# Value products of the first mixer with the values stationary and two heads in column tiles, probabilities divided before the product, and compression in four quadrants of TensorE

## What is computed

```python
p = _split_columns(u @ w_in)                                  # proj blocks and gate blocks
o_a = _stick_breaking(q_a, k_a, v_a)                          # 4 heads: w @ v, w = exp(...) below the diagonal
o_b = _dsa_attention(...)                                     # 4 heads: softmax over the top keys, p @ v_b
o_c = _nsa_attention(...)                                     # 4 heads, three value products, each with a gate:
#   gb[...,0:1] * o_cmp + gb[...,1:2] * o_sel + gb[...,2:3] * o_win
def _compress(tok, pos_emb, w1, w2):                          # for keys and for values, 15 windows of 32 tokens
    hid = gelu(blocks.reshape(B, n_cmp, CMP_LEN * hd) @ w1)   # (15 x 2048) @ (2048 x 128)
    return hid @ w2
def _masked_softmax(s, mask):
    ...
    return e / jnp.maximum(den, 1e-30)
merged = g[0] * (o_a @ w_up[0]) + g[1] * (o_b @ w_up[1]) + g[2] * (o_c @ w_up[2])
return merged @ w_out
```

## Time and profile before

| | us |
|---|---|
| median of 3 runs | 751.03 (749.55 to 751.15) |
| the profiled execution | 750.67 |
| its span | 748.6 |
| PE busy | 741.5 (99%) |
| DVE busy | 601.3 (80%) |
| ACT busy | 376.7 (50%) |
| POOL busy | 30.6 (4%) |

### The profile page before, as it was taken

How to read it: one execution, slowest core, us unless ns; L and a number is a source line. 1 busy time by engine, 2 the same in 40 slices (tenths; PEclk the granted TensorE clock), 3 DMA queues, 4 the chain that set the end, 5 groups by cost and what they waited for, 6 DMA issues and landing times.

```text
span 748.6 us, 14960 instructions
## 1 busy us (share of the span) xinstructions
PE 741.5 (99%) x6348; PEld 732.2 (98%) x6348; DVE 601.3 (80%) x897; ACT 376.7 (50%) x506; POOL 30.6 (4%) x22
## 2 busy tenths in 40 slices
PE   8999999999999999999999999999999999999998
PEld 8999999999999999999999999999999999999998
DVE  4756889899897778998998888979788886687554
ACT  6558255654666543443434666266556553434330
POOL 0000000004000000000000000301110000000000
PEclk9999999999999999999999999999999999999999
DMA  8844373332743459999887526655344565688511
GB/s 334 310 155 154 110 281 113 109 126 102 309 177 138 158 185 365 361 333 338 324 310 276 181 102 225 226 184 210 112 169 142 198 226 176 228 278 303 199 57 57
DMA packets 24113, 156.07 MB, mean 208 GB/s; under 512 B 3568, under 2 KB 3696, under 8 KB 6000
## 3 DMA queue, kind: packets, MB, share of 16 engines
q1 hardware_dynamic: 24048, 155.13, 57.7%
HBM read 154.07 MB, written 1.05 MB: 207 GB/s over the span
## 4 chain that ended last, share of the span: by engine, by line
PE 95%; DVE 2%; DMA 1%; ACT 1%; issue 1%; SPq 0%; DVEq 0%
PE bank L803 17%; PE bank L804 16%; PE bank L805 16%; PE bank L886 9%; PE bank L888 9%; PE bank L889 9%; PE bank L811 3%; PE bank L813 3%; PE bank L814 3%; PE bank L1294 2%; PE bank L1261 1%; DMA sb_raw<-in_stream 1%; PE bank L1271 1%; PE bank L1191 1%; PE bank L1335 0%
## 5 line engine op out<-in xcount | busy, mean ns | idle before, releaser
L1770 DVE TENSOR_TENSOR sb_lo<-sb_raw,sb_hi 128x2048 fp32r<-128x2048 f32 (+1 forms) x114 | 259.2, 2277 | 72.7 <-ACT sb_hi L1425 72.4
L1425 ACT CAST sb_hi<-sb_raw 128x2048 fp32r<-128x2048 f32 (+1 forms) x114 | 215.5, 1895 | 99.6 <-PE bank L889 49.6
L803 PE MATMUL bank<-sb_u_hi,sb_hi 128*128 128x256 f32 (+1 forms) x688 | 193.1, 281 | 0.0
L805 PE MATMUL bank<-sb_u_hi,sb_lo 128*128 128x256 f32 (+1 forms) x688 | 190.5, 277 | 0.0
L804 PE MATMUL bank<-sb_u_lo,sb_hi 128*128 128x256 f32 (+1 forms) x688 | 190.5, 277 | 0.0
L803 PEld LDWEIGHTS bank<-sb_u_hi,sb_hi 128*128 128x128 f32 (+1 forms) x688 | 128.9, 187 | 2.8 <-issue 2.2
L804 PEld LDWEIGHTS bank<-sb_u_lo,sb_hi 128*128 128x128 f32 (+1 forms) x688 | 129.2, 188 | 0.0
L805 PEld LDWEIGHTS bank<-sb_u_hi,sb_lo 128*128 128x128 f32 (+1 forms) x688 | 129.0, 187 | 0.0
L886 PE MATMUL bank<-sb_hid_hi,sb_hi 128*128 128x256 f32 x432 | 119.3, 276 | 0.0
L888 PE MATMUL bank<-sb_hid_lo,sb_hi 128*128 128x256 f32 x432 | 119.2, 276 | 0.0
L889 PE MATMUL bank<-sb_hid_hi,sb_lo 128*128 128x256 f32 x432 | 119.2, 276 | 0.0
(11 more groups left out here) (370 smaller groups left out, 1335.4 us busy)
## 6 DMA issues: line engine op xcount, KB each, us to landing
sb_raw<-in_stream SPq DMA_DIRECT2D x140, 1024.0 KB, 5.2
sb_raw<-in_stream SPq DMA_DIRECT2D x4, 256.0 KB, 6.4
sb_raw<-in_stream SPq DMA_DIRECT2D x2, 512.0 KB, 9.0
sb_mem_t<-in_mem SPq DMA_DIRECT2D x1, 1024.0 KB, 4.8
out<-sb_h SPq DMA_DIRECT2D x4, 256.0 KB, 2.2
sb_const<-in_constants SPq DMA_DIRECT2D x1, 830.0 KB, 11.1
sb_h<-in_x SPq DMA_DIRECT2D x1, 572.0 KB, 3.8
sb_h<-in_x SPq DMA_DIRECT2D x1, 512.0 KB, 6.7
```

The source lines that it names most:

```text
L803: nc.tensor.matmul(out, a_hi, b_hi, start=(i == 0), stop=False)
L805: last = nc.tensor.matmul(out, a_lo, b_hi, start=False, stop=(i == n - 1))
L1425: nc.scalar.copy(place(hi, s)[:, 0:n], x[:, 0:n]).then_inc(sem("hi_ready"), 1)
L1770: tt(place(lo, s)[:, 0:n], x[:, 0:n], f32(place(hi, s)[:, 0:n]), ALU.subtract) \
```

## The change

The table of constants gets `pick`, 16 columns that add the right 16 columns of each 32-row quadrant. Six things change.

1. `pv_stick` runs once for a pair of heads, the values (64 columns) stationary and the weights moving, head 0 into rows 0 to 63 and head 1 into rows 64 to 127 of bank 2, so that the result has features on partitions.
2. `pv_pair(u)` replaces `pv(u)` and `pv(u + 1)` of branches b and c in the same way; the compressed branch (`cmp_pv`) is added into the same bank. `o_group` 0 to 4 and the transposes of `turn_o` go; `turn_o` is now a scaled copy from the bank on ACT and one DVE instruction.
3. The probabilities are divided before they are turned: POOL inverts the sums (and multiplies by the gate for branch c), ACT scales the two halves of each unit.
4. The exponentials, the division and the transposes of a pair of units move into the gate block behind their scores, and `pv_pair` stands right behind that block.
5. `turn_cmp_p` moves from inside gate 7 to behind gate 7, in front of `scores` 8 and 9, and has one more DVE instruction (the division).
6. `cmp_product` is one step with w1 moving (128 columns) and 32 columns of windows stationary, step k in quadrant k mod 4. ACT copies the 128x128 result (`cmp_parts`), and `cmp_sum` adds the quadrants with one product with `pick`. The evacuation of gate 2 moves behind `cmp_product(0)`.

```diff
     block("proj", 7, between=[("suffix", 1)])
-    steps([("pv_stick", 0), ("stick", 2)])
+    steps([("stick", 2)])
...
-    steps([("pv_stick", 1), ("stick", 3), ("split", "gate", 1)])
+    steps([("pv_stick", 0), ("stick", 3), ("split", "gate", 1)])
...
-    steps([("pv_stick", 2), ("split", "gate", 3), ("turn_cmp", 0)])
-    block("gate", 2, between=[("pv_stick", 3), ("o_group", 0), ("turn_cmp", 1), ("index", 0), ("rope1", 3)])
-    steps([("cmp_product", 0, 0)])
-    block("gate", 3, between=[("cmp_product", 0, 1), ("cmp_hidden", 0), ("topk", 0, 0)])
-    steps([("cmp_product", 1, 0), ("topk", 0, 1), ("turn_qk", 2)])
-    block("gate", 4, between=[("cmp_product", 1, 1), ("cmp_hidden", 1), ("cmp_hid",), ("topk", 0, 2)])
+    steps([("split", "gate", 3), ("turn_cmp", 0)])
+    block("gate", 2, evac_now=False, between=[("pv_stick", 2), ("turn_o", 0), ("turn_cmp", 1), ("index", 0), ("rope1", 3)])
+    steps([("cmp_product", 0)])
+    evac(where["gate", 2])
+    block("gate", 3, between=[("cmp_sum", 0), ("cmp_hidden", 0), ("topk", 0, 0)])
+    steps([("cmp_product", 1), ("topk", 0, 1), ("turn_qk", 2)])
+    block("gate", 4, between=[("cmp_sum", 1), ("cmp_hidden", 1), ("cmp_hid",), ("topk", 0, 2)])
...
-    steps([("scores", 4), ("scores", 5), ("topk", 0, 3), ("turn_o", 0)])
+    steps(unit_scores(4) + unit_norms(4) + [("topk", 0, 3)])
     block("gate", 6, ahead=False, between=[("cmp_scores",), ("rounds", "gate", 8)])
-    steps([("turn_p", 4), ("turn_p", 5), ("scores", 6), ("scores", 7)])
-    block("gate", 7, ahead=False, between=[("pv", 4), ("pv", 5), ("turn_cmp_p",), ("split", "gate", 8), ("topk", 1, 0), ("turn_qk", 6)])
-    steps([("turn_p", 6), ("turn_p", 7), ("scores", 8), ("scores", 9), ("topk", 1, 1), ("split", "gate", 9)])
-    block("gate", 8, ahead=False, evac_now=False, between=[("cmp_pv",), ("o_group", 1)])
-    steps([("rounds", "gate", 10), ("pv", 6), ("pv", 7), ("turn_p", 8), ("turn_p", 9), ("scores", 10), ("scores", 11)])
+    steps(unit_scores(6))
+    block("gate", 7, ahead=False, between=unit_turns(4) + unit_norms(6) + [("split", "gate", 8), ("topk", 1, 0), ("turn_qk", 6)])
+    steps([("pv_pair", 4), ("turn_cmp_p",)] + unit_scores(8) + [("topk", 1, 1), ("split", "gate", 9)])
+    block("gate", 8, ahead=False, evac_now=False, between=unit_turns(6) + unit_norms(8) + [("cmp_pv",)])
+    steps([("rounds", "gate", 10), ("pv_pair", 6)] + unit_scores(10))
...
-    block("gate", 11, ahead=False, evac_now=False, between=[("pv", 0), ("pv", 1)])
-    steps([("rounds", "up", 2), ("turn_p", 2), ("turn_p", 3)])
+    block("gate", 11, ahead=False, evac_now=False, between=unit_turns(0) + unit_norms(2))
+    steps([("rounds", "up", 2), ("pv_pair", 0)])
     evac(where["gate", 11])
+    add("turn_o", 2)
     split(where["up", 2])
-    block("up", 0, ahead=False, between=[("merge", 0, 0), ("merge", 0, 1), ("pv", 2), ("pv", 3), ("turn_o", 2),
-                                         ("merge", 0, 2), ("split", "up", 1), ("merge", 0, 3)])
-    block("up", 2, ahead=False, between=[("merge", 1, 0), ("merge", 1, 1), ("rounds", "out", 0), ("turn_o", 1)])
+    block("up", 0, ahead=False, between=[("merge", 0, 0), ("merge", 0, 1)] + unit_turns(2) +
+          [("merge", 0, 2), ("split", "up", 1), ("merge", 0, 3)])
+    steps([("pv_pair", 2), ("turn_o", 1)])
+    block("up", 2, ahead=False, between=[("merge", 1, 0), ("merge", 1, 1), ("rounds", "out", 0)])
...
-            def pv_stick(hd):
+            def pv_stick(first):
...
+                for kt in range(NT):
+                    out, w = (slice(at, at + T), slice(0, T)) if kt == 0 else (slice(at + P, at + T), slice(T, T + P))
+                    for hd in (first, first + 1):
+                        r, c = slice(HD * (hd % 2), HD * (hd % 2) + HD), VA + HD * hd
+                        last = nc.tensor.matmul(ps[r, out], proj[:, kt, c:c + HD], prob[:, hd % 2, w],
+                                                start=(first == kt == 0), stop=(kt == 1), skip_group_check=True)
...
+            def cmp_product(i):
...
+                for k in range(16):
+                    r = slice(32 * (k % 4), 32 * (k % 4) + 32)
+                    pair = 16 * (k - k % 2)
+                    last = nc.tensor.matmul(ps[r, 0:P], cmp_in[:, i, pair:pair + 32], w[:, k, :], start=(k < 4),
+                                            stop=(k >= 12), skip_group_check=True)
+                fill(last, key)
+
+            def cmp_sum(i):
+
+                wait_evacuated(pe, ("cmp_parts", i))
+                ps = claim(("cmp_hidden", i), "turn")
+                fill(nc.tensor.matmul(ps[:, 0:16], cmp_parts[:, i, :], cst("pick"), start=True, stop=True),
+                     ("cmp_hidden", i))
...
+            def pv_pair(u):
...
+                for n, (s, kt) in enumerate(parts):
+                    for x in (u, u + 1):
+                        i = UNITS[x][2]
+                        r = slice(HD * (i % 2), HD * (i % 2) + HD)
+                        p = prob_t_of(x)[:, 0:2 * keys * P].rearrange("p (m k q) -> p m k q", m=2, k=keys)
+                        if kind == "b":
+                            out = ps[r, :].rearrange("p (m t q) -> p m t q", m=2, t=NT)[:, :, t, :]
+                            v, p = proj[:, kt, VB:VB + HD], p[:, :, kt, :]
+                        else:
+                            out = ps[r, i // 2 * T + t * P:i // 2 * T + t * P + P]
+                            v, p = proj[:, kt, (VSEL, VWIN)[s]:(VSEL, VWIN)[s] + HD], p[:, s, kt, :]
+                        last = nc.tensor.matmul(out, v, p, start=(opens and n == 0), stop=(n == len(parts) - 1),
+                                                skip_group_check=True)
...
+            def cmp_product(i):
+
+                key = ("cmp_parts", i)
+                ps = wait_filled(act, key)
+                free(nc.scalar.copy(cmp_parts[:, i, :], ps[:, 0:P]), key)
...
+            def norm_p(u):
+
+                n = P * (UNITS[u][1] + 1)
+                act.wait_ge(sem("rden_ready"), EXP_ORDER[u] - 3)
+                for m in range(2):
+                    x = prob_of(u)[:, m * n:m * n + n]
+                    last = nc.scalar.activation(x, x, ACT.Copy, scale=rden[:, u, m:m + 1])
+                last.then_inc(sem("p_ready"), 1)
...
             def turn_o(c):
-                turn_to((turned_hi[:, :, :], u_hi[:, 2:4, :], u_hi[:, 4:6, :])[c], ("turn_o", c))
+
+                act.wait_ge(sem("pv_done"), (4, 16, 12)[c])
+                if c == 2:
+                    wait_filled(act, ("block", where["gate", 11]))
...
                 link(tt(cmp_d[:, :], cmp_d[:, :], gate_c[:, :, :, 0].rearrange("p t h -> p (t h)"), ALU.mult))
+                heads = p.rearrange("p (h n) -> p h n", n=32)
+                tt(heads, heads, over(cmp_d[:, :], 32), ALU.mult).then_inc(sem("cmp_p_ready"), 1)
```

More of the change, by code:

```diff
@@ L177, in steps @@
             else:
-                if step[0] == "cmp_product" and step[2] == 0:
+                if step[0] == "cmp_product":
                     raw.append(("cmp_w1", step[1]))
@@ L280, in plan @@
+    block("gate", 8, ahead=False, evac_now=False, between=unit_turns(6) + unit_norms(8) + [("cmp_pv",)])
+    steps([("rounds", "gate", 10), ("pv_pair", 6)] + unit_scores(10))
     evac(where["gate", 8])
     steps([("split", "gate", 10), ("topk", 1, 2)])
-    block("gate", 9, ahead=False, evac_now=False, between=[("pv", 8), ("pv", 9)])
-    steps([("rounds", "gate", 11), ("turn_p", 10), ("turn_p", 11), ("scores", 0), ("scores", 1)])
+    block("gate", 9, ahead=False, evac_now=False, between=unit_turns(8) + unit_norms(10))
@@ L284, in plan @@
+    steps([("rounds", "gate", 11), ("pv_pair", 8)] + unit_scores(0))
     evac(where["gate", 9])
     steps([("split", "gate", 11), ("topk", 1, 3)])
-    block("gate", 10, ahead=False, evac_now=False, between=[("pv", 10), ("pv", 11)])
-    steps([("rounds", "up", 0), ("turn_p", 0), ("turn_p", 1), ("scores", 2), ("scores", 3)])
+    block("gate", 10, ahead=False, evac_now=False, between=unit_turns(10) + unit_norms(0))
+    steps([("rounds", "up", 0), ("pv_pair", 10)] + unit_scores(2))
     evac(where["gate", 10])
@@ L1225, in cmp_pv @@
                 wait_evacuated(pe, ("turn_cmp_p",))
-                ps = claim(("o", 1), O_BANK[1])
-                for t in range(NT):
-                    last = nc.tensor.matmul(ps[:, t * T:t * T + T], cmp_in[:, 1, t * P:t * P + P], vc_bd,
-                                            start=True, stop=True)
-                fill(last, ("o", 1))
+                ps = banks[lease["turn_o", 2][0]]
+                for m in range(2):
+                    nc.tensor.matmul(ps[:, m * T:m * T + T], vc_bd[:, m * P:m * P + P], cmp_in[:, 1, :],
+                                     start=False, stop=False, skip_group_check=True)
             def scores(u):
@@ L1272, in turn_p @@
                 fill(last, ("turn_p", u))
+            def pv_pair(u):
+                kind, t, _ = UNITS[u]
```

(31 more changed lines are left out.)

146 lines of the change are left out of this document (71 added, 75 removed).

## The result

| | us |
|---|---|
| median of the changed kernel, 4 runs | 755.9 (755.32 to 756.81) |
| median of before, its runs on the same chip | 750.48 (749.55 to 751.15) |
| ratio | 1.0084, 95% interval 1.0069 to 1.0098 |
| span of the profiled execution | 754.0, before 748.6 |

The change makes the kernel slower by 0.84% (the two medians are 5.4 us apart, a quotient of 1.0072; what is given in us for a ratio further down is worked out from the ratio, 0.84% being 6.3 us). The forecast was 750.5, no change, with a range up to 753.7.

What follows compares the result with a forecast made beforehand. PE, 99% busy, was to wait for ACT and DVE at three points, so out 0 starts 0.5 us earlier: 750.67 less 0.5 is 750.2, plus the median's 0.36 gives 750.5 us, range 747.4 to 753.7.

Steps and rivals of the forecast that it cites:

- A: At `cmp_sum(1)` in gate 4: PE waits about 4 us for ACT's copy behind gate 3's tanh, keeping 0.45 us saved.
- B: At `turn_cmp_p` ahead of gate 8: PE waits 2.3 us for DVE, and gate 8 starts 0.6 us later than before.
- the 0.5 of the sticks: Part of the stick products' saving, 0.5 us, counted toward PE's earlier arrival at `cmp_sum(1)`.
- Column pairs: Value products in two column tiles, priced like row pairs of the scores: 0.65 us for first queries, 1.09 for second.
- Scalings on ACT: Division of the probabilities on ACT, two scalings for each unit, taken at 0.42 us a scaling.
- the clock falls: Rival, 10 of 100: the waits at A and B bring the 1.2 GHz level for half a block, 753.4 us.
- the clock reads below 1.00 behind A: Sign of being wrong: granted clock under full speed after the wait at `cmp_sum(1)`, where the forecast had 1.00.
- Point C: From up 0 to out 0: ACT's late copy for `turn_o(2)` delays DVE's merge; out 0 starts 0.5 us earlier.
- the 3.2 saved: PE's saving after gate 8: 2.34 us of value products and 0.88 us of two `turn_o`.
- Column tiles that take turns: Rival, 15 of 100: products in different column tiles do not run together, so the kernel takes 753.5 us.
- Weight loads not hidden: Rival, 8 of 100: 0.106 us for each of 26 column-tile passes behind B, 2.8 us, giving 751.3 us.
- Every pass removed is time: Rival, 7 of 100: all 8.8 us of PE passes removed come off the time, giving 742.3 us.

Runs made afterwards that it cites:

- e5: The changed kernel with dummy products on PE, 15 ahead of `cmp_sum(1)` in a free bank and 11 ahead of `turn_cmp_p`: 751.97 us, ratio 1.0024.
- e3: The changed kernel with gate 3's evacuation behind `cmp_product(1)` and `turn_cmp_p` back inside gate 7: 749.81 us, ratio 1.0000.
- e6: e3 with ACT's copy of `turn_o(2)` ahead of up 2's rounding and DVE's residues of up 0 ahead of up 2's rest: 748.32 us, ratio 0.9978.
- e7: e2 with the compression of the kernel before (two halves, windows stationary, no quadrants or copy): 749.86 us, ratio 0.9996.
- e9: e7 with the order of e6 behind gate 11 added: 747.65 us, ratio 0.9973.
- e2: The changed kernel with `turn_cmp_p` back inside gate 7, ahead of DVE's rest of gate 8's weights: 750.8 us, ratio 1.0016.
- e1: The changed kernel with the evacuation of gate 3 behind `cmp_product(1)`, so ACT copies the quadrants before the tanh: 752.49 us, ratio 1.0036.
- e8: e6 with nine dummy products in a free bank ahead of the scores of unit 4: 748.49 us, ratio 0.9978.

## Why the prediction was wrong

**The places and the waits were right.** A was forecast as a wait of PE for the copy to `sb_prob_t` of 3.5 to 4.5 us: 3.5. B as 2 to 2.6 us: 2.5. A lies at the edge: the sum had PE at A at 96.2 and it came at 97.0, because the 0.5 of the sticks does not show there (the first compression product starts 22.3 us behind gate 0, before 22.2) and PE stood 0.5 us for DVE ahead of `turn_qk(2)`, a wait that the sum did not have. Both were swallowed by A. PE was to leave `cmp_sum(1)` at 100.65 and left at 101.14; the copy took 0.25 (0.35 taken) but the sum 0.58, already at the lower clock. Column pairs were forecast at 0.65 and 1.09: 0.59 and 1.02. Scalings on ACT 0.42: 0.43 (four in 1.72 to the next start). The sum prices a pair of stick products at 0.85, where its own 0.63 and 0.33 give 0.96; it took 0.81. But for that slip and for the terms below, these rows bear out the working.

**The step that failed is the choice between the forecast and its rival "the clock falls".** I gave 45 to waits with a clock of 1.00 behind them and 10 to a fall, because no row of before showed a gap; and I priced that rival at one half block, 2.9 less 0.5. What happened is that rival twice, on top of the waits: behind A the clock is 0.57 for six microseconds, behind B 0.76. e5 sizes it at 4.5 us; in the profiled executions the stretch from the start of gate 0 to that of out 0 takes 126.15 us in the changed kernel (62.84 to 188.99), 122.1 in e5 (62.39 to 184.50) and 121.0 before (62.95 to 183.92), so the clock is 4.0 of the 5.2 lost. Of these about 2.4 stem from A and 1.6 from B (e5 is 2.4 ahead at gate 8 and 4.0 at gate 9). The wait and the price of a fall were both in the prediction. Forecast waits of 4 and 2.3 us stood beside a clock that I left at full speed, and nothing in the profile of before supported that; "the clock reads below 1.00 behind A" was its own sign of being wrong. The kernel before even places dummy products itself (`stay_warm`, 16 ahead of the first block, from the table `IDLE`), and the prediction did not ask what for.

The Trainium skill, "TensorE: Matmul & The Clock Gate", section "HAM oscillation — how this bites in real kernels", says that gaps in PE's work bring back the slow clock. By that rule the trace agrees at A. The waits that the page tells of are for DMA and last about 3 to 5 us; at B, and in e3 at the scores of unit 4, the clock fell behind shorter ones, of 2.5 and 2.0 us. The rule, weighed as likely rather than as 10 of 100, would have put the forecast on the slower side.

**Point C was mis-sized.** I let gate 8 be 0.6 late and out 0 0.5 early, so 1.1 of the 3.2 saved were to come through. In e5, whose clock is whole, gate 8 starts 1.5 late and out 0 1.1 late, both against the start of gate 0: only 0.4 come through. PE's wait for bank 2 was 1.4, not 0.6: ACT made the copy of `turn_o(2)` at 171.42, 4.4 behind the end of gate 11 at 167.0, where I had 3.9. What the sum left out is the tanh of gate 10, which begins at 164.34, when DVE has delivered, and holds up the copies of units 0 and 1 till 164.88; their transposes were done at 164.1. The rows of ACT in the changed kernel:

```profile
164.34 0.63 ACT L1484 ACTIVATE sb_gates<-sb_gates 128x512 f32<-128x512 f32 x1 [2.80 <-DVE sb_gates L1873]
164.88 0.63 ACT L1681 COPY sb_prob_t<-bank 128x256 f32<-128x256 f32 x2
...
171.42 0.57 ACT L1714 ACTIVATE sb_u_hi<-bank 128x512 fp32r<-128x512 f32 x1
```

e6 shows that this queue is the cause. Together: out 0 came 1.1 late instead of 0.5 early, 1.6 us, and the two falls add 4.0, so 750.2 becomes 755.8; the profiled execution took 756.09.

**B's start was late too.** Gate 7 was to start 1.9 earlier (0.45, 0.44 and 0.98); in e5 it starts 1.2 earlier, against the start of gate 0. Three terms were a little too large: 0.3 at A, 0.1 at `turn_o(0)` and 0.3 at the transposes of units 4 and 5. With the wait of 2.5 for 2.3 that makes gate 8 late by 1.5 instead of 0.6.

**The other rivals.** Column tiles that take turns: refuted, 0.59 where turns would have been 0.88. Weight loads not hidden: refuted. The same row has no room for 0.106 a pass more: it has 0.07 a pass, while each weight load of that line lasts 0.13 us (shortest, median and longest of 60, in ns: 132/137/137). Here the measurement differs from the rule on row groups in Part 3 of "TensorE: Matmul & The Clock Gate" of the Trainium skill, by which the prediction priced this rival. "TensorEngine Tiling (Array Packing)", "Key Properties", of the Trainium skill has tiles run independently, and by that the trace agrees. "Every pass removed is time": refuted by e7 and e9, in which 4 us of passes come back and the kernel is not slower.

What stays open: why the falls differ in length, 6.8 and 3.4 us at A and B of the changed kernel and 3.4 at A in e2 after nearly the same wait, and in e1 and e8 from one execution to the next. A gain of one or two us by an edit that leaves a wait standing can be that.

## What to carry to other kernels

Where PE is 99% busy with another engine at 80 to 90% right behind it, passes taken from PE can turn into waits at the next step that needs the other engine, as they did here, and what counts is where the table puts that step. Price a new idle stretch of PE with the slow stretch that may follow it, compare the mean clocks of all executions before reading the one that has a trace, and test it with dummy products in a bank that nobody holds: they separate the clock from the wait, provided that they do not queue behind the wait themselves. Look in the queue of the engine that delivers (here ACT's copy behind a tanh, and behind a rounding) before taking work off the engine that waits.

## What the runs showed of the hardware

Sixteen products of 128 columns in four quadrants of 32 columns, 32 passes, took 1.01 us in the first compression product, 0.03 a pass, where a whole pass of 128 columns takes 0.11:

```profile
85.17 1.08 PE L1213 MATMUL bank<-sb_raw,sb_cmp_in 128*32 128x128 f32 x32
```

(85.17 to the next start, 86.18.) Four column tiles do run at once. The lower clock behind a wait of TensorE of 3.5 us lasted 6.8 us, in another kernel behind one of 3.4 us only 3.4 us. And a kernel can be made 0.6% faster by 26 products that compute nothing (e5), when PE has 3.5 and 2.5 us to wait.
